# An encoder layer on one core: the products with the values in two column tiles, their row sums on GpSimd

## The reference

```python
s = (jnp.einsum("bqhd,bkhd->bhqk", q_nope, k_nope)
     + jnp.einsum("bqhr,bkr->bhqk", q_rope, k_rope)).astype(jnp.float32) * SM_SCALE
allowed = (k_pos[None, :] // CHUNK) <= (q_pos[:, None] // CHUNK)
s = jnp.where(allowed[None, None], s, jnp.finfo(jnp.float32).min)
p = jax.nn.softmax(s, axis=-1).astype(v.dtype)
return jnp.einsum("bhqk,bkhd->bqhd", p, v)
```

## Time and profile before

| what | value |
|---|---|
| median of 3 runs (lowest, highest) | 1343.79 us (1343.18, 1344.2) |
| the profiled execution: its time, its span | 1344.39 us, 1342.6 us |
| PE busy | 1312.1 us (98%) |
| DVE, ACT busy | 891.2 us (66%), 502.8 us (37%) |
| POOL busy | 57.3 us (4%), 59 instructions |
| the attention stage on PE, first value product to last sample product | 438.0 to 587.3 us of the span |

### The profile page before, as it was taken

How to read it: one execution, slowest core, us unless ns; L and a number is a source line. 1 busy time by engine, 2 the same in 40 slices (tenths; PEclk the granted TensorE clock), 3 DMA queues, 4 the chain that set the end, 5 groups by cost and what they waited for, 6 DMA issues and landing times.

```text
span 1342.6 us, 22926 instructions
## 1 busy us (share of the span) xinstructions
PE 1312.1 (98%) x9288; PEld 1245.7 (93%) x9288; DVE 891.2 (66%) x1391; ACT 502.8 (37%) x833; POOL 57.3 (4%) x59
## 2 busy tenths in 40 slices
PE   6999999999999999999999999999999999999997
PEld 4799999999997677789999999999999999999997
DVE  6699988382655567777885545656456569877743
ACT  5622221234301444346643333333333336444532
POOL 0200000000013122200000000000000000000000
PEclk9899999999999999999999999999999999999999
DMA  9445534711213332030232232331323276455441
GB/s 352 142 142 149 160 116 114 279 37 31 91 30 68 110 78 45 1 100 13 68 101 88 63 110 97 119 103 58 108 88 119 88 275 235 118 178 160 163 138 79
DMA packets 132759, 154.75 MB, mean 115 GB/s; under 512 B 12065, under 2 KB 99705, under 8 KB 130641
## 3 DMA queue, kind: packets, MB, share of 16 engines
q1 hardware_dynamic: 130080, 152.50, 35.8%
q10 hardware_dynamic: 2608, 1.28, 0.4%
HBM read 115.51 MB, written 30.69 MB: 109 GB/s over the span
## 4 chain that ended last, share of the span: by engine, by line
PE 91%; DVE 5%; ACT 1%; issue 1%; DMA 1%; POOL 0%; SPq 0%; ACTq 0%; DVEq 0%; POOLq 0%
PE PS L1360 30%; PE PS L917 18%; PE PS L1426 12%; PE PS L1456 5%; PE PS L1270 4%; PE PS L1123 4%; PE PS L1503 3%; PE PS L1250 3%; PE PS L1308 2%; PE PS L1011 2%; PE PS L1197 2%; PE PS L1217 1%; PE PS L1151 1%; DVE MX L2432 1%; PE PS L886 1%
## 5 line engine op out<-in xcount | busy, mean ns | idle before, releaser
L1360 PE MATMUL PS<-HBL_T,EH 128*128 128x264 f32 x640 | 169.3, 285 | 0.0
L1360 PE MATMUL PS<-HBH_T,EH 128*128 128x264 f32 x640 | 169.1, 284 | 0.0
L917 PE MATMUL PS<-HH,WH 128*128 128x352 f32 x432 | 139.7, 324 | 1.6 <-DVE CQ L2299 0.8
L917 PE MATMUL PS<-HL,WH 128*128 128x352 f32 x432 | 139.0, 323 | 0.0
L1360 PE MATMUL PS<-HBH_T,EL 128*128 128x264 f32 x640 | 130.4, 285 | 0.0
L1360 PE MATMUL PS<-HBL_B,EH 128*128 128x264 f32 x480 | 127.5, 286 | 0.0
L1360 PE MATMUL PS<-HBH_B,EH 128*128 128x264 f32 x480 | 127.1, 285 | 0.0
L1360 PEld LDWEIGHTS PS<-HBH_T,EH 128*128 128x128 f32 x640 | 120.6, 188 | 0.0
L1360 PEld LDWEIGHTS PS<-HBL_T,EH 128*128 128x128 f32 x640 | 120.3, 188 | 0.0
L1426 PE MATMUL PS<-DTH,DWH 128*128 128x264 f32 x440 | 116.6, 286 | 0.1
L1426 PE MATMUL PS<-DTL,DWH 128*128 128x264 f32 x440 | 116.7, 285 | 0.0
(11 more groups left out here) (346 smaller groups left out, 3166.4 us busy)
## 6 DMA issues: line engine op xcount, KB each, us to landing
ADA<-in_w_ada SPq DMA_DIRECT2D x22, 1024.0 KB, 6.0
DTR<-saved_operands SPq DMA_DIRECT2D x66, 264.0 KB, 2.9
HALF_W<-in_w_gate SPq DMA_DIRECT2D x22, 512.0 KB, 4.0
saved_operands<-UP SPq DMA_DIRECT2D x10, 1056.0 KB, 4.0
RAW<-in_w_in SPq DMA_DIRECT2D x20, 512.0 KB, 6.6
DWR<-in_w_down SPq DMA_DIRECT2D x33, 256.0 KB, 3.2
HALF_W<-in_w_up SPq DMA_DIRECT2D x12, 512.0 KB, 3.7
saved_operands<-TB SPq DMA_DIRECT2D x11, 528.0 KB, 4.8
```

The costliest lines, as they stand in the source:

```text
L917: mm = pe.matmul(PS[:, b + n, 0:CH], w, x[k][:, n * CH:(n + 1) * CH], start=(first and w is weights[0][k] and x is xs[0]), stop=(last and ...
L1360: mm = pe.matmul(PS[:, 2 * s + n, 0:HQ], w, x[:, k, n * HQ:(n + 1) * HQ], start=(first and w is wh and x is xh), stop=(ends and w is wl), ...
```

## The change

The value products are made in two column tiles. The stationary side is now 64 columns of V instead of 128, and the query tiles of even and odd number go to different halves of the partitions of bank 4, as two products that may run beside each other. Each key tile has a buffer of its own for its probabilities (PT1 to PT7, and two of ACC0 for tile 0). The sums are no longer a by-product: GpSimd adds the seven other tiles of a head onto ACC0, and one pair of products with a block of ones (`sums`) makes the row sums from it. values(h, i) stands one slot later, two slots behind its scores; `sums` of a head stands in slot 1 of the next. The row of maxima goes by DMA straight into the operand, with VectorE writing it rounded, and GpSimd's round_maxima and QTM are gone. ScalarE copies outputs and sums later.

```diff
-        PP = at("PP", [P, 2, D], F32, B)
+        PT = {i: at(f"PT{i}", [P, S - P * i], F32, at_byte) for i, at_byte in
+              ((1, B), (2, B + 3584), (5, B + 6656), (3, 4 * U), (4, 4 * U + 2560), (6, 4 * U + 4608), (7, 4 * U + 5632))}
...
-        QTM = at("QTM", [P, T], F32, 4 * U)
+        ACC0 = at("ACC0", [P, 2, D], F32, 8 * U + 16384)
...
-        MROW = at("MROW", [P, 2, P], F32, o + 33792)
+        MROW = at("MROW", [P, 2, P], F32R, o + 33792)
...
+        def row_tiles(ap, first):
+
+            return ap.rearrange("p (t c) -> p t c", c=P)[:, first::2, :]
+
+        def tile_half(h, parity):
+
+            e = (h + parity) % 2
+            return slice(VH * e, VH * (e + 1))
...
             def load_maxima(h):
 
                 sp.wait_ge(m_kept, h + 1)
-                if h >= 1:
-                    sp.wait_ge(max_rounded, h)
-                sp.dma_start(QTM[PLAIN:CONTRACT, 0:S].rearrange("o (t q) -> o t q", t=KD),
-                             MROW[0:KD, h % 2, :]).then_inc(max_rows, 16)
...
+                if h >= 2:
+                    sp.wait_ge(s_full, STEPS * (h - 1))
+                sp.wait_ge(rounded, 2 * h + 1)
+                row = QTH[h % 2][PLAIN:CONTRACT, :].bitcast(F32)
+                sp.dma_start(row[:, 0:S].rearrange("o (t q) -> o t q", t=KD),
+                             MROW[0:KD, h % 2, :].bitcast(F32)).then_inc(max_rows, 16)
...
                 if i == 0:
-                    pe.wait_ge(max_rounded, h + 1)
+                    pe.wait_ge(max_rows, 32 * (h + 1))
                     pe.wait_ge(head_lo, 2 * (h + 1))
...
+            def probabilities(h, i):
+
+                return ACC0[:, h % 2, :] if i == 0 else PT[i][:]
+
             def values(h, i):
...
-                        pe.wait_ge(o_kept, 3 * h)
-                    for bank, lo, hi, stop in ((4, q0, 512, 3), (5, max(q0, 512), S, KD - 1)):
-                        if lo < hi:
-                            mm = pe.matmul(PS[:, bank, lo % 512:hi - 512 * (bank - 4)], V[:, i, h // 2, VH * (h % 2):VH * (h % 2) + P],
-                                           PP[:, n % 2, lo - q0:hi - q0], start=(i == 0), stop=(i == stop))
...
+                        pe.wait_ge(o_kept, 3 * h - 2)
+                    for parity in ((0, 1), (1, 0))[i % 2]:
+                        t = i + (i + parity) % 2
+                        if t < KD:
+                            mm = pe.matmul(PS[tile_half(h, parity), 4, P * (t // 2):512], V[:, i, j, P * e:P * e + VH],
+                                           row_tiles(probabilities(h, i), t - i), start=(i == 0), stop=(i == KD - 2 + parity))
+                    mm.then_inc(p_used if i < KD - 1 else o_full, 1)
...
+            def sums(h):
+
+                pe.wait_ge(p_added, (KD - 1) * (h + 1))
+                pe.wait_ge(o_kept, 3 * h + 2)
+                for parity in range(2):
+                    mm = pe.matmul(PS[tile_half(h, parity), 5, :], V[:, 0, 0, VH:2 * VH], row_tiles(ACC0[:, h % 2, :], parity),
+                                   start=True, stop=True)
+                mm.then_inc(o_full, 1)
...
                         score_maxima(h + 1, (i, 0))
-                    values(h, i)
+                    if i == 1 and h >= 1:
+                        sums(h - 1)
+                    if i >= 1:
+                        values(h, i - 1)
+                    elif h >= 1:
+                        values(h - 1, STEPS - 1)
                     if h + 1 < HEADS:
                         score_maxima(h + 1, (i, 1))
+            values(HEADS - 1, STEPS - 1)
+            sums(HEADS - 1)
...
-                elif 0 < i < KD and n >= 2:
-                    act.wait_ge(p_used, (KD - 1) * h + i - 1)
...
+                elif 0 < i < KD and h >= 1:
+                    if i < KD - 1:
+                        act.wait_ge(p_used, (KD - 1) * (h - 1) + i + 1)
+                    else:
+                        act.wait_ge(o_full, 3 * h - 2)
+                    act.wait_ge(p_added, (KD - 1) * (h - 1) + i)
...
                     exponentials(h, i)
-                keep_output(h, 0)
...
+                    if i <= 2 and h >= 1:
+                        keep_output(h - 1, i)
...
                 if h + 1 < HEADS:
                     exponentials(h + 1, 0)
-                keep_output(h, 2)
+                keep_output(h, 0)
+            for n in (1, 2):
+                keep_output(HEADS - 1, n)
...
-                dve.wait_ge(o_kept, 3 * HEADS - 1 + t)
+                dve.wait_ge(o_kept, 3 * HEADS)
...
-            def round_maxima(h):
-
-                pool.wait_ge(rounded, 2 * max(h, 1) + 2)
-                if h >= 1:
-                    pool.wait_ge(max_rounded, h)
-                pool.wait_ge(max_rows, 32 * (h + 1))
-                pool.tensor_copy(QTH[h % 2][OWN:CONTRACT, :], QTM[OWN:CONTRACT, :]).then_inc(max_rounded, 1)
+            def add_probabilities(h, i):
+
+                n = (KD - 1) * h + i - 1
+                if i == 1:
+                    pool.wait_ge(p_used, n + 1)
+                pool.wait_ge(exp_done, STEPS * h + i + 1)
+                if n >= 1:
+                    pool.wait_ge(p_added, n)
+                pool.tensor_tensor(ACC0[:, h % 2, P * i:], ACC0[:, h % 2, P * i:], PT[i][:], ALU.add)\
+                    .then_inc(p_added, 1)
...
-            round_maxima(0)
-            for h in range(1, HEADS):
-                round_maxima(h)
-                if h + 1 < HEADS:
+            for h in range(HEADS):
+                if 1 <= h < HEADS - 1:
                     round_head(h + 1)
+                for i in range(1, KD):
+                    add_probabilities(h, i)
```

More of the change, by code:

```diff
@@ L398, in build @@
         head_lo = sem("head_lo")
[L399 removed]
+        p_added = sem("p_added")
         m_full = sem("m_full")
@@ L1750, in exponentials @@
                 act.wait_ge(s_full, n + 1)
[L1751 removed]
+                if i == 0 and h >= 2:
+                    act.wait_ge(o_full, 3 * h - 3)
+                elif 0 < i < KD and h >= 1:
+                    if i < KD - 1:
+                        act.wait_ge(p_used, (KD - 1) * (h - 1) + i + 1)
+                    else:
+                        act.wait_ge(o_full, 3 * h - 2)
+                    act.wait_ge(p_added, (KD - 1) * (h - 1) + i)
+                elif i == KD and h >= 1:
                     act.wait_ge(o_full, 3 * h - 1)
[L1753 to L1756 removed]
                 if i < KD:
                     nq = S - P * i
[L1759 removed]
+                    dst = ACC0[:, h % 2, :] if i == 0 else PT[i][:]
+                    act.activation(dst, PS[:, b:b + 2, :].rearrange("p b q -> p (b q)")[:, 0:nq], ACT.Exp,
                                    scale=SCALE).then_inc(exp_done, 1)
@@ L1769, in keep_output @@
                 rows = slice(NOPE * e, NOPE * (e + 1))
-                t = (slice(0, 512), slice(512, S), slice(S, T))[part]
-                src = PS[:, (4, 5, 4)[part], 0:t.stop - t.start]
                 act.wait_ge(o_full, 3 * h + part + 1)
@@ L1774, in keep_output @@
                     act.wait_ge(ao_lo, j - 1)
-                act.activation(OP[j % 2][rows, t], src[rows, :], ACT.Copy)
-                act.activation(SUMS[j % 2][rows, t], src[VH * (1 - e):VH * (2 - e), :], ACT.Copy).then_inc(o_kept, 1)
+                if part == 1:
+                    act.activation(OP[j % 2][rows, S:T], PS[rows, 5, 0:SD], ACT.Copy)
+                    ins = act.activation(SUMS[j % 2][rows, S:T], PS[VH * (1 - e):VH * (2 - e), 5, 0:SD], ACT.Copy)
+                else:
+                    dst, bank = ((OP[j % 2], 4), None, (SUMS[j % 2], 5))[part]
+                    for parity in range(2):
+                        ins = act.activation(row_tiles(dst[rows, 0:S], parity),
+                                             PS[tile_half(h, parity), bank, :].rearrange("p (t c) -> p t c", c=P), ACT.Copy)
+                ins.then_inc(o_kept, 1)
             def round_ao(m):
@@ L1784, in _ @@
             for h in range(HEADS):
-                for i in range(1, 5):
+                for i in range(1, STEPS):
                     exponentials(h, i)
-                keep_output(h, 0)
-                for i in range(5, STEPS):
-                    exponentials(h, i)
-                    if h == HEADS - 1 and i < STEPS - 1:
+                    if i <= 2 and h >= 1:
+                        keep_output(h - 1, i)
+                    if h == HEADS - 1 and 5 <= i < STEPS - 1:
                         if i == 5:
```

32 lines of the change are left out of this document (9 added, 23 removed).

## The result

The changed kernel takes 1379.16 us (median of 3 runs, 1374.69 to 1380.43) against 1343.79: 1.026 times as long (95% interval 1.022 to 1.029). The forecast was 1353 within 1340.5 to 1361. It had the sign, and was too low by 26 us.

A forecast was written before the change was run, and what follows sets the result against it. It took PE to bound an attention head, with POOL and DVE close behind. Terms of 8.2 + 0.7 - 0.7 - 1.0 + 0.9 + 0.8 gave +8.9 us on 1344.39, forecast as 1353, range 1340.5 to 1361.

The forecast's parts named there:

- a later KTL: In heads without a scaled output, DVE's low part of the keys (KTL) comes 1.9 us later, behind POOL's additions.
- POOL and DVE in turns: Main forecast, chance 0.62: POOL's additions and DVE's two-SBUF-input instructions hold each other up; 1353 us, range 1347 to 1361.
- The heads with a scaling: Heads 3 and 5, where DVE scales an output: 23.6 us against 19.46, 8.2 us more for the two.
- The heads without one: Heads without a scaled output: POOL's path takes 19.6 us until the next n0 (first maxima product), against 19.4; just fits.
- The additions: POOL's seven additions per head, 3584 columns, take 8.3 us; bounds 3.6 to 9.2 us.
- Changes of the tiled form: TensorE going in and out of column tiles costs 0.22 us a group, eight groups, 1.8 us a head.
- switches of 0.4 us: Dearer tiled-form changes, 1.4 us a head more where PE limits: 1356 to 1361, upper part of the main forecast.
- n1's wait: Second maxima product (n1) waits for DVE's reduction of the first: PE stands some 0.7 us more in seven heads.
- heads 1 and 2: These heads carry one more DVE instruction, nine rows of QTL: 0.7 us once.
- The end of the stage: Last head saves 1.0 us, its sums wait about 0.9 for the last addition, the output projection 0.8 for DVE.
- Tiles that overlap: The two column tiles of value products run beside each other: 5.1 us a head with sums, before changes of form.
- the rival without overlap: Rival: tiles do not run beside each other, 1378 us, half overlap 1361; chance 0.08 for no or half overlap.

The follow-up runs named there:

- x1_no_adds: Changed kernel with GpSimd additions of 16 columns each instead of 896 to 128: 1351.01 us, 1.006 times the kernel before.
- x16_fill_more: x11_fill with three more waits of TensorE filled by products whose results are overwritten: 1364.93 us, 1.016 times the kernel before.
- x14: x1_no_adds with the maxima placed as in x5_both and the value products in five groups instead of eight: 1352.94 us.
- x5_both: Changed kernel with queries and keys rounded on ScalarE from head 2 on, and n1 and later maxima products one place later: 1355.65 us, 1.011 times the kernel before.
- x11_fill: Changed kernel with 49 products more, their results overwritten, put where TensorE would stand still: 1369.89 us, 1.019 times the kernel before.
- x8_one_tile: x1_no_adds with both value products of a pair in the same half of the partitions, so they can't overlap: 1371.91 us, 1.020 times the kernel before.
- x2_half_adds: Changed kernel with half the columns of each GpSimd addition: 1355.37 us, 1.009 times the kernel before.
- x7_before_adds: Kernel before, without column tiles, plus GpSimd additions of the same sizes in a spare tile: 1366.33 us, 1.016 times the kernel before.

## Why the prediction missed

The stage can be cut in three for the four kernels that settle it: first scores of the stage to the n0 near 457 us, five heads from there, and the rest up to the output projection's first product (us, each from starts of records):

| | to n0 | five heads | rest | sum |
|---|---|---|---|---|
| before | 23.0 | 97.2 | 32.9 | 153.1 |
| x1_no_adds: products alone | 22.0 | 99.5 | 35.7 | 157.2 |
| x16_fill_more: all the work, clock held in the heads | 23.7 | 110.4 | 37.8 | 172.0 |
| changed kernel | 25.0 | 122.0 | 39.7 | 186.7 |

So of 33.6 us, 4.1 are the products, 14.8 POOL's additions with the waits that they make, and 14.7 the clock. The forecast's terms for the same three were -2.3 (0.3 less in seven heads, 1.0 less in the last, 0.8 behind), some 11 (the rest of its +8.9), and nothing. The profiled execution as a whole lost 34.8 us (1344.39 to 1379.16). The cut is not quite clean: each row is one execution, x1's the fastest of five (its median is 2.5 us longer); x16's fill costs up to 0.6 us in three heads, and its last wait still costs some clock.

**The step that failed was one that the sum did not have.** The forecast added up waits at full clock, "PE stands for some 0.7 us more", and took every duration on PE as fixed. It isn't: behind many waits of 0.6 to 2.8 us the products that follow run at half the rate for some microseconds. The forecast had most of these waits (n1, n0 at h = 4 and 6, the sums, a later KTL) but no price for what comes behind them; that price, some 15 us, is as large as what the additions cost by their waits. Nothing in the profile of before warned of it within the stage, since PE had no such wait there; its granted clock was 1.00. But a row at the front of that same trace did:

```profile
56.26 0.75 PE L1011 MATMUL PS<-HH,WH 128*128 128x352 f32 x3 [1.72 <-ACT HH L1593]
```

From 57.0 to 60.3 us, right behind this wait of 1.72 us, the granted clock is 0.50. In the changed kernel the same wait, of 1.72 us too, kept 1.00: one such row could have put the price on the list, though not its size.

**POOL and DVE in turns: right.** The heads with a scaling were forecast at 23.6 us; x16_fill_more shows 23.8 twice. The heads without one were said to just fit, at 19.6 us; the terms written there add up to 19.1, and x16_fill_more takes 20.6, with n0 at 498.99 right behind POOL's KTH (497.66 + 1.28). The additions were put at 8.3 us a head by themselves; with what they wait for DVE they fill 11.5 us of POOL. One row sums them over the five heads of the changed kernel (length, POOL; mean of the five):

```profile
sum 122.03, POOL 57.45; mean POOL 11.49
```

The timeline of DVE in a head with a scaling of the changed kernel answers to the earlier trace rows: QTL 1.24 is now 2.16, KTL 1.51 is 2.59, the scaling's product 1.24 is 2.04:

```profile
520.91 2.16 DVE L2483 TENSOR_TENSOR QTL<-QT,QTH 96x1056 fp32r<-96x1056 f32 x1
523.00 2.59 DVE L2489 TENSOR_TENSOR KTL<-KT,KTH 64x1312 fp32r<-64x1312 f32 x1
525.51 2.04 DVE L2503 TENSOR_TENSOR OP<-OP,SUMS 128x1056 f32<-128x1056 f32 x1
```

**Changes of the tiled form: mis-sized.** 0.22 us was taken from one group; x14 gives 0.34 against x1 and 0.30 against x5_both. For 64 groups the difference is 5 to 8 us, 0.6 to 1.0 a head, most of what makes a head 19.9 us in x1 instead of 19.1. It lay within the bounds given (0 to 0.4), and the prediction put switches of 0.4 us at 1356 to 1361.

**n1's wait, and heads 1 and 2: right in kind.** 0.62 us measured for 0.7. The additional QTL of heads 1 and 2 was put at 0.7 us once; the two waits for KTL are 0.85 and 1.22 us (1.11 and 1.24 in x11_fill).

**The end of the stage: too cheap.** The last sums wait 2.1 us for the last addition, forecast 0.9; the rest of x1_no_adds (a head with maxima, the last head, and what follows) is 2.8 us longer than before, where the forecast had -0.3, -1.0 and 0.8; of these 3.3 us, two heads' changes are 1.3 to 2.0.

**Tiles that overlap: right**, by x8_one_tile.

With 5 to 8 us for the changes and 2 to 3 for the end, the forecast's own sum would have been some 1360 to 1364, near what the kernel takes when its waits are filled (1364.9). The other 14 us are the clock. That the measured 1379.16 lies next to the 1378 of the rival without overlap is chance: the tiles do overlap.

## What to carry to other kernels

A wait on TensorE is not priced by its length alone: where it stood nearly without a gap before, first ask whether the clock stays, and give each new wait of about a microsecond a second price, what the following products lose at half rate, with a chance that it comes due; a few idle products in the wait show within one run how much that is. Regrouping products for fewer changes of the tiling moves the work that hides other engines; where all of it hides something, the changes have to stay. And work given to GpSimd is paid twice when VectorE works with two SBUF inputs: both queues grow (here 8.3 to 11.5 us of additions, and 1.24 to 2.16 us for QTL).

## What the runs showed of the hardware

The granted clock fell behind gaps that were much shorter than expected: single waits of 0.9 to 2.8 us, and in x2_half_adds one of 0.62. Not every one did it. The traced execution of x1_no_adds has one of 1.3 us and six of 0.62 and keeps 1.00, as does x16_fill_more with three of 0.6; in x7_before_adds a stretch with waits of 0.9 and 1.1 us stayed at 1.00, and one with 1.53 fell. Nor does the length alone decide: the wait of 1.32 us before n1 of head 1 is the same in the changed kernel, x1_no_adds and x11_fill, and the clock fell behind it (at 440.2 us) in the first alone; the waits for KTL of 1.11 and 1.24 us in x11_fill brought it down, those of 1.09 and 1.34 in x5_both did not. The Trainium skill, in TensorE: Matmul & The Clock Gate, A second HAM failure mode, describes a kernel whose short idle times between groups of products make the clock swing; the runs here agree (0.82 to 0.93 in the heads of the changed kernel), and add that idle products cure it (1379 to 1365 us). Where the limit lies and what else counts stays open; no run varied one wait alone.

That fill makes a kernel faster is the second surprise: 65 products that compute nothing, and the whole is 14 us shorter, with the same work on POOL and DVE.
